# Hybrid RG-LRU / neighbourhood-attention / MoE step: the first expert's down weights are loaded later in the sync engine's queue

## The chip, the cores and the metric

One core of one Trainium2 chip. The metric is the device time of one execution of the whole program, in microseconds (us); the median of several runs is given. The engines are TensorE (PE in the profile, PEld for its weight loads), VectorE (DVE), ScalarE (ACT), GpSimd (POOL) and SyncE (SP), which here only issues DMAs.

## The reference

One layer for 128 context tokens and 512 latent tokens with D_MODEL = 1024, all in float32. The part that matters here is the end, a mixture of 16 experts of which every token uses two:

```python
scores = jax.nn.sigmoid((t @ w_router).astype(jnp.float32))
...
_, idx = lax.top_k(masked, TOP_K)
...
for e in range(N_EXPERTS):
    a = jax.nn.silu(t @ w_exp_gate[e]) * (t @ w_exp_up[e])
    y = y + combine[:, e:e + 1] * (a @ w_exp_down[e])
```

Ahead of it stand adaLN modulation, one input projection, the RG-LRU branch, the attention branch and the merge with its output projection; behind it a gated residual and a final RMSNorm. Gate and up weights of an expert are 1024 x 512, down weights 512 x 1024, so each of the three is 2 MB in float32.

## The kernel before

The program has one stream of instructions for each engine, written out by hand, and semaphores between them. An engine runs its own stream in order, so an instruction that waits holds all that stand behind it.

**Precision.** Every matmul operand is split in two parts: ScalarE makes the high part (a copy to the fp32r type), VectorE or GpSimd the low part (the difference), and TensorE sums three products, high x high, low x high and high x low.

**The expert stage.** The 640 tokens are sorted by expert. A slot tile is 128 rows for one expert. Routing (VectorE, after the output projection) gives each token its slots, and a list idxI of the token in each slot. The normed rows hrow (5 tiles of 128 x 1024) are made by TensorE transposes and ScalarE, get their shift on VectorE (line 1780), and are written by SyncE to h_rows in DRAM (line 543). GpSimd then waits for idxI (idx_ok) and for all five stores (hrow_out) and issues an indirect DMA for each slot tile, which gathers 128 rows of h_rows into one of two buffers hS (line 634 for the first two tiles, line 629 for all later ones). Meanwhile TensorE turns x1 into rows too (line 906), which ScalarE evicts to x1t (line 1257).

**One slot tile on TensorE.** Eight transposes turn hS into columns (line 935), ScalarE takes the high part hSH (line 1268), VectorE the low part hSL (line 1889). Then come the gate product, the up product and, one tile behind, the transposes of the activation (line 956) and the down product; all products are on line 943. For the first tile the gate product is cut in two halves, with the transposes of the second tile's hS between them.

**Expert weights.** Wg, Wu and Wd are one raw buffer each; `load(x, t, ex)` on SyncE waits until VectorE has made the low part of the tile before (W_lo_ok[x] >= t) and then issues one 2 MB DMA; x is 0 for gate, 1 for up, 2 for down. Expert 0's gate weights are loaded earlier, by `first_gate`, in two halves. ScalarE makes the high parts in two pieces of 4 k-tiles each (line 1241), VectorE the low parts in two pieces (line 1883).

**Who reads expert 0's down weights.** On ScalarE the order is: the high part of tile 0's rows, a wait for the row stores, the down weights, then expert 0:

```python
h_high(0, 0)
act.wait_ge(hrow_out, 16 * TT)
weights_high(2, 0)
expert(0, 0, 0)
```

On VectorE it is the low part of the up weights, that of the rows, that of the down weights, then expert 0. The down product of expert 0 itself is taken by TensorE after the up product of expert 1.

Of the kernel before, what the change touches and what calls it, by code (L numbers as in the profile page):

```python
# [106 lines left out]
def build(nc, xT, cT, w_ada, w_ada_late, b_ada, norm_g, final_g, wtiles, par_in, pack, biasd, w_router, r_bias,  # L107
# [235 lines left out]
    def wait(eng, s, v):  # L343

        if not (isinstance(v, int) and v <= 0):
            eng.wait_ge(s, v)
# [72 lines left out]
    def _(sp):  # L419
# [109 lines left out]
        def load(x, t, ex):  # L529

            wait(sp, W_lo_ok[x], t)
            sp.sem_inc(ticks, 1)
            sp.dma_start(Wraw[x][:], experts[bass.ds(ex, 1), x].rearrange("o p (k f) -> (o p) k f", k=KT)) \
                .then_inc(W_in[x], 16)

        sp.wait_ge(half_mm, 2 * (N1 + N2 + N3))
        load(1, 0, 0)
        load(2, 0, 0)
        sp.wait_ge(g2T_ok, 1)
        sp.dma_start(g2d, g2T[0:2 * KT, :]).then_inc(g2_out, 16)  # L540
        for t in range(TT):
            sp.wait_ge(slot_ok, t + 1)
            sp.dma_start(h2d[t * P:(t + 1) * P, :], hrow[:, t, :]).then_inc(hrow_out, 16)
        load(0, 1, 1)
        for x in (1, 2):
            load(x, 1, 1)
        def rows_out(t, b):
# [1504 lines left out]
```

## Time and profile before

| | us |
|---|---|
| median of 3 runs | 1198.25 (1197.57 to 1202.51) |
| time of the profiled execution | 1198.25 |
| its span, first to last instruction | 1196.3 |
| TensorE busy | 1107.3 |
| VectorE busy | 909.7 |
| ScalarE busy | 678.9 |

The profile is of one execution. Times within it are counted from the start of its span; the 1.95 us between time and span lie around the instructions. A busy engine is one that has an instruction in it, and TensorE's busy time includes matmuls that wait in its pipeline. A DMA is seen as its issue on an engine's queue (SPq, POOLq), as its packets, and as its landing, when its semaphore is raised. Queue q1 carries the DMAs that SyncE issues, q0 those that GpSimd issues. The granted clock (PEclk) is a share of 2.4 GHz: 1.00 is that level and 0.50 is 1.2 GHz.

### The profile page before, as it was taken

Reading aid. Unit: us, or ns where it says so; the run is one execution under the profiler, and the core shown is the slowest. Engines: PE = TensorE matmul, PEld = TensorE weight load, DVE = VectorE, ACT = ScalarE, POOL = GpSimd, SP = SyncE. Lnnn points to the kernel's source line nnn. Section 1 sums busy time; section 2 is a strip of 40 time slices with the busy share of each in tenths; the row PEclk is TensorE's granted clock in tenths of the full one; section 3 lists DMA queues with packets and bytes.
Section 4 is the critical chain, followed back from the end, with each engine's and each line's share of the span. In section 5 each row is a group of like instructions: output and inputs, shape, how many; then the busy total and the mean of one; then the engine's idle time right before and its main releaser. Section 6 shows DMA issues by size and latency. Waiting matters only on the chain.

```text
span 1196.3 us, 19808 instructions
## 1 busy us (share of the span) xinstructions
PE 1107.3 (93%) x7082; PEld 1014.9 (85%) x7082; DVE 909.7 (76%) x1255; ACT 678.9 (57%) x1041; POOL 256.1 (21%) x139
## 2 busy tenths in 40 slices
PE   5999999999999999999999999995999999999950
PEld 1599999999999998899999999995788888888840
DVE  6748797978879796866556637558799998999928
ACT  3646757666666756642222212455688877877824
POOL 0132222122222122233333323201110110110011
PEclk9899999999999999999999999997999999999985
DMA  9235412212111221134444445538799999999945
GB/s 366 98 113 160 148 48 81 72 67 84 56 63 57 79 69 50 41 130 152 140 140 141 140 148 192 173 114 316 291 396 421 424 411 418 405 414 427 366 151 200
DMA packets 54569, 232.17 MB, mean 194 GB/s; under 512 B 5328, under 2 KB 22000, under 8 KB 46064
## 3 DMA queue, kind: packets, MB, share of 16 engines
q1 hardware_dynamic: 50480, 216.79, 48.2%
q0 software_dynamic: 4032, 14.68, 3.2%
q8 instruction: 29, 0.48, 0.2%
q14 instruction: 28, 0.23, 0.1%
HBM read 210.45 MB, written 21.00 MB: 193 GB/s over the span
## 4 chain that ended last, share of the span: by engine, by line
PE 50%; DVE 4%; ACT 1%; issue 1%; DMA 1%; POOL 0%; DVEq 0%; SPq 0%; ACTq 0%; POOLq 0%
PE PS L943 24%; PE PS L710 21%; PE PS L935 1%; PE PS L815 1%; PE PS L956 1%; PE PS L860 1%; DVE xo L1947 1%; DVE xo L1949 1%; DVE hrow L1780 0%; PE PS L906 0%; DMA G<-slot_rows,slotI 0%; DVE yo L1959 0%; DVE WgLo L1883 0%; DVE acc L1604 0%; PE PS L848 0%
## 5 line engine op out<-in xcount | busy, mean ns | idle before, releaser
L604 POOL TENSOR_TENSOR wLo<-wRaw,wHi 128x1024 fp32r<-128x1024 f32 x80 | 202.9, 2537 | 547.3 <-ACT wHi L1020 547.2
L710 PE MATMUL PS<-hHi,wHi 128*128 128x320 f32 x896 | 285.2, 318 | 4.3 <-DVE hLo L1435 1.9
L710 PE MATMUL PS<-hLo,wHi 128*128 128x320 f32 x896 | 277.4, 310 | 0.0
L710 PE MATMUL PS<-hHi,wLo 128*128 128x320 f32 x896 | 277.4, 310 | 0.0
L710 PEld LDWEIGHTS PS<-hHi,wHi 128*128 128x128 f32 x896 | 169.4, 189 | 5.6 <-issue 3.2
L710 PEld LDWEIGHTS PS<-hLo,wHi 128*128 128x128 f32 x896 | 169.1, 189 | 0.0
L710 PEld LDWEIGHTS PS<-hHi,wLo 128*128 128x128 f32 x896 | 168.8, 188 | 0.0
L1604 DVE SCALAR_TENSOR_TENSOR acc<-adaL,csil,acc 128x512 f32<-128x512 f32 x112 | 103.8, 985 | 10.3 <-DMA adaL<-in_w_ada_late 9.9
L1020 ACT ACTIVATE wHi<-wRaw 128x1024 fp32r<-128x1024 f32 x80 | 84.1, 1051 | 44.8 <-PE PS L710 44.7
L1883 DVE TENSOR_TENSOR WgLo<-Wg,WgHi 128x2048 fp32r<-128x2048 f32 x34 | 76.4, 2287 | 13.0 <-ACT WgHi L1241 12.9
L1883 DVE TENSOR_TENSOR WdLo<-Wd,WdHi 128x2048 fp32r<-128x2048 f32 x34 | 76.4, 2288 | 9.5 <-ACT WdHi L1241 9.2
L1883 DVE TENSOR_TENSOR WuLo<-Wu,WuHi 128x2048 fp32r<-128x2048 f32 x36 | 80.8, 2286 | 2.6 <-ACT WuHi L1241 2.5
L1459 DVE TENSOR_TENSOR PtLo<-PS,PtHi 128x384 fp32r<-128x384 f32 (+1 forms) x80 | 39.7, 496 | 52.4 <-ACT PtHi L1056 52.3
L1470 DVE TENSOR_SCALAR Sb<-Sb,prec 128x384 f32<-128x384 f32 (+1 forms) x80 | 70.6, 925 | 1.4
L1120 ACT ACTIVATE Sb<-Sb,nmax 128x384 f32<-128x384 f32 (+1 forms) x80 | 45.0, 564 | 46.6 <-DVE nmax L1482 46.5
L1241 ACT ACTIVATE WgHi<-Wg 128x2048 fp32r<-128x2048 f32 x34 | 63.3, 1911 | 11.9 <-DMA Wg<-in_experts 11.8
L1241 ACT ACTIVATE WuHi<-Wu 128x2048 fp32r<-128x2048 f32 x36 | 66.8, 1908 | 3.3 <-DMA Wu<-in_experts 2.0
L1056 ACT ACTIVATE PtHi<-PS 128x384 fp32r<-128x384 f32 (+1 forms) x80 | 35.6, 444 | 56.7 <-PE PS L790 56.0
L626 POOL COPY idxc<-idxI 128x1 int32 (+1 forms) x16 | 20.3, 1269 | 216.5 <-PE PS L935 216.5
L1241 ACT ACTIVATE WdHi<-Wd 128x2048 fp32r<-128x2048 f32 x34 | 63.0, 1905 | 0.0
L943 PE MATMUL PS<-WgHi,hSH 128*128 128x512 f32 x144 | 56.9, 395 | 4.0 <-DVE hSL L1889 2.4
L943 PE MATMUL PS<-WuHi,hSH 128*128 128x512 f32 x144 | 57.8, 402 | 0.0
(324 smaller groups left out, 2764.9 us busy)
## 6 DMA issues: line engine op xcount, KB each, us to landing
wRaw<-in_wtiles SPq DMA_DIRECT2D x80, 512.0 KB, 3.4
Wu<-in_experts SPq DMA_DIRECT2D x18, 2048.0 KB, 9.4
Wg<-in_experts SPq DMA_DIRECT2D x18, 2048.0 KB, 9.7
Wd<-in_experts SPq DMA_DIRECT2D x17, 2048.0 KB
adaL<-in_w_ada_late SPq DMA_DIRECT2D x32, 512.0 KB, 4.3
slot_rows<-Ys SPq DMA_DIRECT2D x18, 512.0 KB, 10.7
ada<-in_w_ada SPq DMA_DIRECT2D x8, 1024.0 KB, 17.7
slot_rows<-tab SPq DMA_DIRECT2D x10, 512.0 KB, 6.5
```

The source lines that it names most:

```text
L604: nc.gpsimd.tensor_tensor(wLo[b][:], wRaw[b][:], wHi[b][:].bitcast(F32), ALU.subtract).then_inc(w_lo, 1)
L626: seq.step(nc.gpsimd.tensor_copy(idxc[b][:], idxI[:, bass.ds(t, 1)]))
L710: r = mm(PS[:, bank, 0:HALF], w[:, k, :], x[:, k, cols], start=(k == 0 and w is wHi[b] and x is xh), stop=(k == KT - 1 and w is wLo[b]))
L943: x = mm(out, lhs[l][:, k, :], rhs[r](k)[:, cols], start=(k == 0 and l == r), stop=(k == n - 1 and l == 1))
L1020: A(wHi[b][:], wRaw[b][:], ACT.Copy).then_inc(w_hi, 1)
L1056: A(PtHi[:, 0:nt, hh * P:(hh + 1) * P], PS[:, 6, 0:nt * P].rearrange("p (t q) -> p t q", q=P), ACT.Copy).then_inc(pt_hi, 1)
L1120: A(Sb[(blk + b) % 2][hh][:, 0:w], Sb[(blk + b) % 2][hh][:, 0:w], ACT.Exp, scale=-1.0, bias=nmax[hh][:], accum_out=psumr[:, hh:hh + 1]).th ...
L1241: A(W_hi[x][:, k:k + 4], Wraw[x][:, k:k + 4], ACT.Copy).then_inc(W_hi_ok[x], 1)
L1459: v.tensor_tensor(PtLo[:, 0:nt, cols], PS[:, 6, 0:nt * P].rearrange("p (t q) -> p t q", q=P), PtHi[:, 0:nt, cols].bitcast(F32), ALU.subtra ...
L1470: v.tensor_scalar(x, x, prec[:, hh:hh + 1], None, ALU.mult).then_inc(prob_ok, 1)
L1604: y = v.scalar_tensor_tensor(acc[:, g, :], w, c1, acc[:, g, :], ALU.mult, ALU.add)
L1883: y = v.tensor_tensor(W_lo[x][:, k:k + 4], Wraw[x][:, k:k + 4], W_hi[x][:, k:k + 4].bitcast(F32), ALU.subtract)
```

## The change

On SyncE, the load of expert 0's down weights, `load(2, 0, 0)`, is issued after the gate load of expert 1 and so after the store of g2 and the five stores of the rows. It was issued right behind the up load of expert 0. No other instruction is changed.

```diff
         sp.wait_ge(half_mm, 2 * (N1 + N2 + N3))
         load(1, 0, 0)
-        load(2, 0, 0)
         sp.wait_ge(g2T_ok, 1)
         sp.dma_start(g2d, g2T[0:2 * KT, :]).then_inc(g2_out, 16)
         for t in range(TT):
             sp.wait_ge(slot_ok, t + 1)
             sp.dma_start(h2d[t * P:(t + 1) * P, :], hrow[:, t, :]).then_inc(hrow_out, 16)
         load(0, 1, 1)
+        load(2, 0, 0)
         for x in (1, 2):
             load(x, 1, 1)
```

## Rows read from the trace of the kernel before

**Rows 1.** The page: TensorE's busy time, share of the span, instructions.

```profile
PE 1107.3 (93%) x7082; PEld 1014.9 (85%) x7082; DVE 909.7 (76%) x1255; ACT 678.9 (57%) x1041; POOL 256.1 (21%) x139
```

**Rows 2.** Busy by stretch: length, PE, PEld, DVE, ACT, POOL, granted clock, DMA share, GB/s.

```profile
815.00:822.00 7.00, 3.24 (x25) 2.91 (x25) 6.30 (x25) 5.53 (x6) 0.30 (x1) 0.74 0.99 369
822.00:827.00 5.00, 4.39 (x21) 3.99 (x19) 4.96 (x7) 3.56 (x6) 3.48 (x2) 0.54 0.53 146
850.00:1140.00 290.00, 290.00 (x1376) 241.22 (x1376) 263.02 (x163) 229.53 (x164) 34.67 (x28) 1.00 0.98 399
```

**Rows 3.** The chain that ended last, 780 to 880 us: start, length, what.

```profile
821.19 5.22 PE PS L906 x24
826.43 0.61 ACT x1t L1257
...
827.08 1.11 PE PS L935 x8
...
830.55 4.34 PE PS L943 x12
834.90 0.88 PE PS L935 x8
...
839.05 1.92 ACT WgHi L1241
...
845.63 5.71 PE PS L943 x24
```

**Rows 4.** Timeline of the SP queue and of POOL, 797 to 850: start, length, what.

```profile
798.17 0.36 SPq L533 DMA_DIRECT2D Wd<-in_experts  x1
...
808.25 6.64 SPq L543 DMA_DIRECT2D h_rows<-hrow  x5
815.00 0.36 SPq L533 DMA_DIRECT2D Wg<-in_experts  x1
827.27 0.33 SPq L533 DMA_DIRECT2D Wu<-in_experts  x1
...
821.70 1.11 POOL L634 DMA_INDIRECT hS<-h_rows,idxI  x1 [36.16 <-DVE idxI L1863]
```

**Rows 5.** Gathers' issue to landing: first; first two; 829.22; 836.81; 14 later.

```profile
DMA to landing us min/median/max: 5.1/5.1/5.1
...
DMA to landing us min/median/max: 5.1/5.6/6.0
...
DMA to landing us min/median/max: 8.2/8.2/8.2
...
DMA to landing us min/median/max: 8.7/8.7/8.7
...
DMA to landing us min/median/max: 9.0/10.9/12.3
```

**Rows 6.** Queues (packets, MB, share): 797:809.3, 815:822.5, 822.5:826, 829:833, 884:888.

```profile
q1 hardware_dynamic: 292, 4.11, 86.2%
...
q1 hardware_dynamic: 302, 2.68, 95.7%
...
q0 software_dynamic: 141, 0.52, 46.7%
...
q1 hardware_dynamic: 87, 1.43, 92.4%
...
q0 software_dynamic: 95, 0.38, 23.1%
```

**Rows 7.** Busy by stretch, columns as in rows 2.

```profile
827.00:830.00 3.00, 1.10 (x8) 0.86 (x8) 0.90 (x2) 1.81 (x3) 0.96 (x2) 1.00 0.74 251
830.00:833.00 3.00, 2.45 (x6) 1.97 (x7) 2.43 (x2) 2.84 (x2) 0.17 (x1) 0.50 1.01 404
```

**Rows 8.** Timeline of ScalarE, 820 to 848; idle before and what ended it.

```profile
829.14 3.70 ACT L1241 ACTIVATE WdHi<-Wd 128x2048 fp32r<-128x2048 f32 x2
835.81 1.03 ACT L1268 ACTIVATE hSH<-PS 128x1024 fp32r<-128x1024 f32 x1 [2.97 <-PE PS L935]
```

## The prediction

> **What bounds the kernel now.** I read first the page's line of TensorE [rows 1]: it is busy for 93% of the span, so what is to be found is where it isn't. The busy times by stretch say where. From 850 to 1140 us, which is nearly the whole expert loop, TensorE is busy 290.0 of 290.0 us and the DMA engines move 399 GB/s; between 815 and 827 us TensorE is far from full and its clock is down [rows 2]. So the loop runs at TensorE's own pace and nothing before it is made up in it: a shift of the first expert by x us is a shift of the end by x us. The question is what the change does to the start of the loop.
>
> The chain of work that ended last shows what sets that start [rows 3]. Routing ends on VectorE and in a few small matmuls; then TensorE transposes x1 (24 in 5.22 us, to 826.41) and ScalarE evicts the last of them until 827.04. Then come the eight transposes of the first tile of gathered rows at 827.08, their high and low parts on ScalarE and VectorE, and the first gate product of expert 0 at 830.55. The gate is done in two halves, with the second gather's transposes between them at 834.90; when it has ended, ScalarE splits the next gate weights from 839.05, VectorE takes their low part, and expert 1 begins at 845.63. Every piece after 827 hangs on the one before it, without a transfer among them.
>
> Beside this chain stands the first gather (hS buffer 0). GpSimd issues it at 821.70 [rows 4] and it takes 5.1 us to land [rows 5], which is 826.8. TensorE takes it up at 827.08, right behind the eviction that ended at 827.04. So gather and eviction end together: the gather has 0.3 us of slack and no more. That is the wait which decides this case.
>
> **The change part by part.** *Taken from 798.17.* The load of expert 0's down weights (2 MB) leaves the first burst. Before, it was issued 0.44 us after the up weights, and h_rows follow from 808.25 [rows 4]. An emptier queue can only make those row stores land sooner. The last is issued at 808.25 + 6.64 - 0.32 = 814.57, and the gather is issued at 821.70, when the token list (idxI) is there; the stores had 7 us. I cost this gain at 0. Even a gather that landed at once would gain only 827.08 - 827.04 = 0.04 us, as the eviction is there.
>
> *Added behind the next gate load.* SP issues the gate load of expert 1 at 815.00; the moved load now follows at about 815.4, with no semaphore to wait for. The next instruction on SP waits for the low part of the up weights and goes out at 827.27 [rows 4] as before, so SP's own queue loses nothing.
>
> *What the transfer does there.* From 815 to 822.5 us queue q1 moved 2.68 MB, which is the last row store and the gate tile, with the engines' share at 95.7% [rows 6]. That is 0.36 MB/us; in a stretch of weights alone (829 to 833) it is 1.43 MB in 4 us, the same. From 797 to 809.3 the up load and the moved one made 4.11 MB [rows 6], over the 10.3 us after the first data (1.3 us behind the issue of 797.7, an estimate) 0.40. The moved 2.10 MB (2048 KB) thus take 2.10/0.40 = 5.2 us behind the gate tile's end at about 822.4, and q1 is full until 827.6. The gather of 821.70 was the one transfer of before that met a queue about to run dry. Now it meets five more microseconds of work.
>
> *The price of that for the gather.* Three kinds of rows bound it. The one before took 5.1 us, which is the lower end (no loss). The second and third gathers after it, issued at 829.22 and 836.81 with one weight tile in flight each, took 8.2 and 8.7 us; the 14 of the loop, where stores of Ys and more than one tile are in flight, took 9.0 to 12.3, median 10.9 [rows 5]. I take the middle of the first two, 8.5, as their load is the nearest: a gather issued some 2 to 6 us ahead of the tile's end. It lands at 821.70 + 8.5 = 830.2 and TensorE's transposes begin there instead of 827.08: +3.1 us. Where these us go is seen from 829 to 833: only q1 moved, 1.43 MB, and not one packet of the gather issued at 829.22 [rows 6], which so stood still for 3.8 of its 8.2 us. Ends for the forecast: a landing at 829.8 (+2.7, the 8.2 rounded down), and 831.4 (+4.3): no packet before q1 runs dry at 827.6, and then the 3.8 us that the first gather took from 823.0, with q1 empty, to its landing at 826.8.
>
> *The clock.* TensorE's granted clock was 1.00 from 827 to 830, where it did 1.10 us of work, and 0.50 from 830 to 833 [rows 7]: the first matmuls of the gate ran at the level of 1.2 GHz. With the gather late TensorE idles 3 us more ahead of the eight transposes. At the low level 24 transposes took 5.22 us [rows 3], so eight take 1.74 against 1.11: +0.6. The gate's first half took 4.34 us for 12 matmuls [rows 3]. In the loop 1376 of them and of the transposes take 290 us [rows 2], 0.21 us each, so 12 take 2.5 at full clock and 5.1 at half: here some 8 were slow. If the fall comes sooner, so may the rise, and two fewer are slow (-0.4); or all 12 are and a few of the second half (+1.0). I take +0.9 for transposes and gate together, with ends of -0.4 and +1.6.
>
> *What stays hidden.* The down weights are first read by ScalarE at 829.14, right behind hSH [rows 8]. They land at about 827.6 plus what the gathers take from them, some 829 to 830, while ScalarE, with the gather late, comes to them at 829.14 + 3.1 = 832.2 or after. Were the gather not late they would cost up to 1 us there, but ScalarE then idled 2.97 us before the next hSH [rows 8]: cost 0. With that cover gone it would be the lateness less 2.97. The second gather took 6.0 us [rows 5] and went out within 2 us of the first, so it landed before 830; it is needed at 834.90 [rows 3], and that moment moves with the first. Four us later is still in time. The up weights of expert 1, issued 827.27, are first read after the gate weights' split, past 843. The copy of g2 is read at the very end.
>
> *Sum.* 3.1 (gather) + 0.9 (clock) - 0 (row stores) = +4.0 us, made against the profiled execution's 1198.25 us (span 1196.3), which is also the median of the three runs: 1202.25, say 1202.2. The forecast's own range is +2.3 (2.7 - 0.4) to +5.9 (4.3 + 1.6), 1200.5 to 1204.2.
>
> The Trainium skill, "DMA: Bandwidth & Descriptors", section "Queues, rings and completion order", says that each DMA engine takes turns between the rows of queues it has work for, a packet at a time. By that rule alone the gather would begin to move at once, between the packets of q1, and not stand still; the third rival gives what this would make. The trace agrees for a gather that has begun (from 884 to 888, 95 packets of q0 passed beside q1's [rows 6]) and not for its first 4 us.
>
> **The rivals.**
> (1) *The gather fares as in the loop.* It would land 10.7 to 12.3 us after its issue, at 832.4 to 834.0: +5.3 to +6.9, with the clock's 0.9 +6.2 to +7.8, that is 1204.5 to 1206. For it: at 821.7 two tiles are queued, not one, the second gather follows in 1.4 us, and the up load of 827.27 begins as the first gather should be catching up. Against: no store of Ys is in flight, and q1 has a gap after 827.6. It decides from 10.5 us between issue and landing. This is the rival of the other side, slower than the measurement's bound.
> (2) *No cost.* The gather's packets go ahead of the moved tile, or that tile's engines are free early; it lands by 827.1: 1198.3. For it: the first gather took 5.1 us though the gate tile was in flight for its first 0.7. Against: all 16 gathers after the first two took 8.2 or more [rows 5], and each had a tile in flight.
> (3) *Turns from the start.* The gather never stands still but shares. From 822.5 to 826 q0 moved 141 packets [rows 6], 40 a us, so the 128 rows of the first gather took 3.2 of its 5.1 us. At the 24 a us of 884 to 888 they take 5.3: 5.1 + 2.1 = 7.2 us, landed at 828.9, +1.8, and with 0.3 for the clock +2.1: 1200.4. For it: the first gather had queue 1's last 0.7 us beside it and lost little. Against: the 4 us without one packet. It decides if packets of q0 are seen before 825.
>
> **How the numbers follow.** About 0.5% (6 us) is what a measurement of this kernel can tell from no change. Forecast 0.56 (of it 0.04 past +6 us); rival 1 0.18 (0.17 past); rival 2 0.12; rival 3 0.10; and 0.04 for what none of them names, of which 0.03 I give to a gain, for which the eviction at 827.04 leaves no room that I can find. With 0.01 of rival 2 this makes faster 0.04, same 0.74, slower 0.22. The predicted time is the forecast's, 1202.2. The range takes in rival 2 below and the greater part of rival 1 above: 1198.0 to 1205.5.
>
> **What would show it.** In the changed kernel's profile: the moved load at about 815.4 on SP; q1 busy until 827 or 828; the first gather with about 8.5 us to landing in place of 5.1, and TensorE's first eight transposes of hS waiting for a DMA, not for ScalarE; the first gate product at about 834 to 835 in place of 830.55; expert 1 at 849 to 850 in place of 845.63; ScalarE not waiting for the down weights; and TensorE full from there. The prediction is wrong if the gather still lands by 827.1, if expert 1's start moves by another amount than the gather, or if the loop makes up the shift.

## The result, and the profile after

The changed kernel takes 1206.29 us (median of 13 runs) against 1199.91 of the kernel before (13 runs): a ratio of 1.0065 with a 95% interval of 1.0048 to 1.0082, so +5.8 to +9.8 us. The two medians are 6.4 us apart, a ratio of 1.0053; the ratio takes in more runs, 39 of the changed kernel with a median of 1207.37. Two further measurements of the same pair gave 1.0063 (1.0037 to 1.0090) and 1.0051 (1.0026 to 1.0076); the kernel before against itself gave 1.0018 (0.9995 to 1.0041) and 1.0011 (0.9984 to 1.0037). Over the three measurements the loss is 6.1 to 7.8 us. Forecast were +4.0 us and 1202.2, with a range up to 1205.5, and slower by over 0.5% had a chance of 0.22.

First the queues' timeline of the changed kernel. All times of this profile stand 3.7 us later than those of before already at the up load (801.47 for 797.73), which is taken up below; so times are read from the first gather's issue.

```profile
811.99 6.64 SPq L542 DMA_DIRECT2D h_rows<-hrow  x5
818.76 0.35 SPq L533 DMA_DIRECT2D Wg<-in_experts  x1
819.22 0.72 SPq L533 DMA_DIRECT2D Wd<-in_experts  x1
830.99 0.33 SPq L533 DMA_DIRECT2D Wu<-in_experts  x1
...
825.42 1.11 POOL L634 DMA_INDIRECT hS<-h_rows,idxI  x1 [36.13 <-DVE idxI L1863]
```

The moved load is where it was looked for, 0.46 us behind the gate load, and 6.2 us ahead of the gather. The next view is the landing of that gather, with the packets of the queues from 825 to 829 (two lines) and from 829 to 833 (two lines).

```profile
DMA to landing us min/median/max: 8.4/8.4/8.4
...
q1 hardware_dynamic: 118, 1.67, 97.6%
q14 instruction: 1, 0.01, 0.5%
...
q1 hardware_dynamic: 66, 0.82, 48.8%
q0 software_dynamic: 197, 0.75, 47.2%
```

The gather was issued at 825.42, and up to 829 there is not one packet of q0: q1 fills the engines to 97.6% with the moved weights. Then q0 passes. It lands after 8.4 us, where it took 5.1 before [rows 5]. The Trainium skill, "DMA: Bandwidth & Descriptors", section "Queues, rings and completion order", has each engine take turns between queues by packets. The trace agrees from 829 on, and not for the 3.6 us before; by turns from the start the forecast had 7.2 us. Not all of the 3.6 us is the moved load's: in the kernel before, where q1 ran dry, the first packet of q0 is seen between 823.2 and 823.7 too, 1.5 to 2 us after the issue.

The chain that ended last now runs through the gather, which was not in it before [rows 3]:

```profile
825.42 8.45 DMA hS<-h_rows,idxI
...
834.01 1.96 PE PS L935 x8
...
838.32 5.40 PE PS L943 x12
843.72 0.87 PE PS L935 x8
...
847.87 1.92 ACT WgHi L1241
...
854.45 5.73 PE PS L943 x24
```

Counted from the gather's issue (821.70 before), TensorE's transposes begin at 8.59 us for 5.38 (+3.21); they take 1.96 for 1.11 (+0.85); the gate's first half takes 5.40 for 4.34 (+1.06); the pieces between are equal to 0.02. Expert 1 begins at 29.03 for 23.93: +5.10. The busy times by stretch, with the columns of [rows 2], show what the second and third terms are:

```profile
834.00:836.00 2.00, 1.94 (x8) 1.55 (x8) 0.00 (x0) 0.02 (x1) 0.00 (x0) 0.50 0.98 414
836.00:838.00 2.00, 0.00 (x0) 0.00 (x0) 0.96 (x1) 2.00 (x2) 1.14 (x2) 0.50 0.96 410
838.00:842.00 4.00, 3.68 (x9) 2.91 (x10) 3.43 (x3) 2.60 (x2) 0.00 (x0) 0.50 0.58 213
842.00:844.00 2.00, 2.00 (x10) 1.56 (x9) 1.33 (x1) 0.00 (x0) 0.00 (x0) 0.63 0.00 0
```

The clock is at 0.50, the level of 1.2 GHz, through both the transposes and nearly all of the gate's first half. Ahead of them TensorE had waited for the gather, with 0.04 us of work from 830 to 834. Before, the clock was 1.00 at the transposes, 0.50 from 830 to 833 [rows 7], 0.80 from 833 to 834 and 1.00 after. ScalarE's timeline answers to [rows 8]:

```profile
836.90 3.70 ACT L1241 ACTIVATE WdHi<-Wd 128x2048 fp32r<-128x2048 f32 x2
844.63 1.03 ACT L1268 ACTIVATE hSH<-PS 128x1024 fp32r<-128x1024 f32 x1 [4.03 <-PE PS L935]
```

It comes to the down weights right behind hSH and waits for nothing; they had landed 13.7 us after their issue, at 832.9. Behind expert 1's start the two profiles run alike: 351.05 us to the end for 350.67. The moved weights are thus not late themselves; they make the gather late.

How much slack the gather had before is less fixed than the 0.3 us of the prediction. In the third of six profiles of the kernel before, issued at the same 821.70, it landed after:

```profile
DMA to landing us min/median/max: 4.4/4.4/4.4
```

The six landings are 4.4, 4.4, 4.5, 4.6, 5.1 and 5.1 us, while TensorE began on it 5.38 or 5.39 us after the issue in five of them: there the eviction of x1 set the start, and the slack was 0.3 to 1.0 us.

### The profile page after: what moved, and what is told of

Its sections match the earlier page's. It is cut to its first block, busy times and chain, and to the rows that moved or that the text cites. A ratio compares the mean times of both kernels' runs of the same rounds, so it can differ in the third digit from the quotient of the medians.

```text
span 1205.5 us, 19808 instructions
## 1 busy us (share of the span) xinstructions
PE 1111.0 (92%) x7082; PEld 1018.0 (84%) x7082; DVE 911.6 (76%) x1255; ACT 679.6 (56%) x1041; POOL 257.6 (21%) x139
## 4 chain that ended last, share of the span: by engine, by line
PE 50%; DVE 4%; DMA 1%; issue 1%; ACT 1%; POOL 0%; DVEq 0%; SPq 0%; ACTq 0%; POOLq 0%
PE PS L943 24%; PE PS L710 21%; PE PS L935 1%; PE PS L815 1%; DMA hS<-h_rows,idxI 1%; PE PS L860 1%; PE PS L956 1%; DVE xo L1947 1%; DVE xo L1949 1%; DVE hrow L1780 0%; DVE yo L1959 0%; DMA G<-slot_rows,slotI 0%; PE PS L848 0%; DVE WgLo L1883 0%; DMA slot_rows<-Ys 0%
```

## The experiments

**The same load one place ahead.** If the down weights' own lateness cost, loading them ahead of the gate weights would help; if the bytes in the queue cost, it would not.

```diff
-        load(0, 1, 1)
         load(2, 0, 0)
+        load(0, 1, 1)
```

> The moved load stands one place ahead: behind the row stores, but before the gate load of expert 1. Queue theory: the same bytes are queued when the gather is issued, so the gather takes 8.0 to 9.0 us and expert 1 begins about 29 us after the gather's issue; ratio 1.004 to 1.008, the same as the changed kernel. Rival (the down weights come too late for ScalarE, which holds the next high parts): they land 5 us earlier here, so the loss should go, ratio 0.998 to 1.002.

Ratio 1.0056 (1.0029 to 1.0082). In the chain:

```profile
822.45 8.21 DMA hS<-h_rows,idxI
...
830.80 1.96 PE PS L935 x8
...
851.57 3.00 PE PS L943 x12
```

The gather takes 8.2 us and expert 1 begins 29.12 us after its issue. The order of the two loads makes no difference in these profiles; that both are in the queue when the gather comes is common to them.

**The same load behind the gather's landing.**

```diff
         load(0, 1, 1)
+        sp.wait_ge(hs_in[0], 16)
         load(2, 0, 0)
```

> As the changed kernel, but SyncE waits for the landing of the first gather before it issues the load of the down weights (and with it the up load of expert 1). The down weights land later still, at about 833 us on the clock of the kernel before. Queue theory: the gather meets only the gate tile and takes 5 us, TensorE's transposes begin 5.4 us after its issue, and ScalarE's wait for the down weights, some 4 us, is covered by the 4.7 us that it idles before the tanh of the gate: expert 1 begins 23.9 to 24.5 us after the gather's issue, ratio 0.999 to 1.002. Rival (late down weights cost): the loss is as large as in the changed kernel or larger, ratio 1.004 or above, with ScalarE waiting for Wd and the first gate product on time.

Ratio 1.0037 (1.0013 to 1.0061). The chain, and below it ScalarE's timeline:

```profile
824.82 4.31 DMA hS<-h_rows,idxI
...
829.21 8.29 DMA Wd<-in_experts
...
850.30 6.58 PE PS L944 x21
...
837.59 3.73 ACT L1242 ACTIVATE WdHi<-Wd 128x2048 fp32r<-128x2048 f32 x2 [5.23 <-DMA Wd<-in_experts]
```

The queue's part came out: without the moved tile the gather takes 4.3 us, and TensorE's transposes begin 5.38 us after its issue, to the hundredth as before. The rest of my expectation was wrong by a piece. The down weights took 8.3 us to land, not the 5.2 of their bytes, ScalarE waited 5.23 us for them, and expert 1 began at 25.48 for 23.93 us, 1.55 late. ScalarE's idle time of 4.7 us is not a full cover: VectorE's low part of the down weights (4.49 us) then stands in front of its work for the next rows and gate weights, and holds the chain. So down weights that keep ScalarE waiting for 5.23 us cost 1.55 us. The changed kernel does not reach it. The ratio, +1.6 to +7.3 us, is above the 0.999 to 1.002 expected, and it can't tell the two theories apart: its profile had 352.7 us from expert 1 to the end and the stall that is taken up below. What speaks for the queue is the stage.

**Half of it.** K-tiles 0 to 3 of the down weights in the old place, 4 to 7 in the new. ScalarE's waits are set to match (not shown).

```diff
         load(1, 0, 0)
-        load(2, 0, 0)
+        sp.dma_start(Wraw[2][:, 0:4], experts[0, 2].rearrange("p (k f) -> p k f", k=KT)[:, 0:4]) \
+            .then_inc(Wl_in, 16)
...
         load(0, 1, 1)
+        sp.dma_start(Wraw[2][:, 4:8], experts[0, 2].rearrange("p (k f) -> p k f", k=KT)[:, 4:8]) \
+            .then_inc(W_in[2], 16)
```

> Half of the down weights (k-tiles 0 to 3, 1 MB) is loaded in the old place, half in the new. Queue theory: q1 runs dry 2.6 us after the gate tile's end and not 5.2; the gather stands still until its packets' turn and takes 6.5 to 8 us; expert 1 begins 26 to 27.5 us after the gather's issue; ratio 1.002 to 1.005. If a gather always stands still for its 4 us whenever any tile is queued behind the running one, it takes 8 us as with the whole tile, and the ratio is that of the changed kernel. Rival (late down weights): the second half still lands before ScalarE comes to it, ratio 1.000.

Ratio 1.0038 (1.0014 to 1.0062).

```profile
822.65 5.79 DMA hS<-h_rows,idxI
...
828.57 1.08 PE PS L938 x8
...
832.01 5.49 PE PS L946 x12
...
848.41 5.72 PE PS L946 x24
```

The gather takes 5.8 us, less than the 6.5 to 8 expected, and TensorE begins on it 0.54 us later than before. Half of the bytes cost a sixth of the delay (0.54 for 3.21), so the gather does not wait in proportion to the bytes. The time at which q1 runs dry fits better. After the gather's issue q1 still moved 0.25 MB in the kernel before, until some 1.5 us after it, 1.2 MB here, until about 4, and 2.2 MB in the changed kernel, until about 7. The last two gathers land 1.5 to 2 us after that. The half load's q1 is dry before even a gather with nothing beside it has landed (4.4 us, in a run below), so its bytes cost little. This is read from three profiles, and no run tests it. Of the loss of 1.83 us at expert 1, 1.15 are the gate's first half, 5.49 us for 4.34: the slow clock once more. But the kernel before has 5.49 in one of its six profiles too, so this part can't be put down to the half load.

**Keeping TensorE busy.** Transposes of the identity are added where TensorE waits, into PSUM columns that nobody reads. The third of the four places, ahead of the first gather's transposes, is used in the changed kernel only.

```diff
+        def warm(n, bank):
+            for _ in range(n):
+                nc.tensor.transpose(PS[:, bank, 0:P], C("ident"), C("ident"))
...
         to_rows(0, xa, range(2 * TT))
+        warm(36, 0)
...
         to_rows(1, x1, range(4))
+        warm(14, 0)
...
         pe.wait_ge(tr_ev, 4 * TT)
+        warm(36, 4)
...
         h_cols(0, 0, 16)
+        warm(14, 4)
         expert(0, 0, 16)
```

> The changed kernel, with transposes of the identity added on TensorE where it waits: 36 behind the first transposes to rows, 14 ahead of the inverse list, 36 before the first gather's transposes, 14 between these and the first gate product; they write PSUM columns that nobody reads. Clock theory: of the changed kernel's loss 0.9 us in the eight transposes and 1.1 in the gate's first half come from the low clock at the restart; here the granted clock stays 1.00, the eight transposes take 1.1 us, the first 12 gate matmuls under 3.2, and expert 1 begins 25 to 26.5 us after the gather's issue instead of 27.3 to 29.1; ratio to the kernel before 1.001 to 1.004. Rival (the whole loss is the gather's landing, the clock's share is noise): expert 1 at 28 to 29, ratio 1.006. The gather itself must stay at 8 to 9 us by both.

Ratio 1.0026 (1.0003 to 1.0049).

```profile
823.24 8.84 DMA hS<-h_rows,idxI
...
832.12 1.11 PE PS L943 x8
...
835.59 3.02 PE PS L951 x12
...
849.34 5.73 PE PS L951 x24
```

The gather is as late as ever (8.8 us), but the transposes take 1.11 us and the 12 matmuls 3.02. Expert 1 begins 26.10 us after the gather's issue where the changed kernel has 27.30 to 29.44. Against a kernel before that has no such transposes, what is left is 2.2 us: the gather's +3.5 less the 1.3 that the gate gains.

> The kernel before with the same transposes of the identity, save the 36 that stand before the first gather's transposes. Clock theory: the first 12 gate matmuls take under 3.2 us instead of 4.3 and the transposes of x1 run at full clock, so that the gather alone ends the wait: expert 1 begins 22 to 23 us after the gather's issue, 1 to 2 us sooner, ratio 0.998 to 1.000. Rival: no gain, 23.9 us as before, as the added transposes hold TensorE up when the rows come.

Ratio 0.9995 (0.9975 to 1.0014), which is no difference that can be told.

```profile
827.40 1.11 PE PS L942 x8
...
830.87 3.06 PE PS L950 x12
...
844.65 5.69 PE PS L950 x24
```

Expert 1 begins 22.64 us after the gather's issue for 23.93, so 1.3 us are gained in the stage, as expected of the gate (3.06 for 4.34). The transposes of x1 did not get faster, against the expectation: 24 in 5.22 us as before. The gain is below what the ratio can show.

Set side by side, these two kernels give the price of the moved load with the low clock out of both: expert 1 at 26.10 for 22.64 us, +3.46, and TensorE's start on the gather at 8.88 for 5.39, +3.49. So the gather is all that is left of the loss, and what the changed kernel lost beyond it was the clock.

> As before_warm, and SyncE issues expert 1's gate load only when the first gather has landed, so that the gather meets no weight tile at all. Queue theory: the gather takes 4.0 to 4.5 us instead of 5.1, and expert 1 begins another 0.5 to 0.8 us sooner if the gate weights, which then land some 8 to 9 us after their issue at about 826, are there when ScalarE comes to them 17 us after the gather's issue. Ratio 0.997 to 1.000. Rival: they are late for ScalarE, and expert 1 begins at 24 us or later.

Ratio 1.0003 (0.9984 to 1.0021). SyncE waits here for the first gather before it loads expert 1's gate weights.

```profile
820.42 4.36 DMA hS<-h_rows,idxI
...
842.61 11.67 DMA Wg<-in_experts
...
862.72 7.34 PE PS L951 x24
```

The gather takes 4.4 us, which is no gain: it took 4.5 in the run above. Expert 1 begins at 22.2 us, 0.4 sooner still, and that comes from elsewhere. TensorE begins on the gather 4.50 us after its issue for 5.39, as the granted clock was 1.00 from 820 to 824.9 and the transposes of x1 ended sooner; then the 14 added transposes held the gate up by 0.8 us. Later the gate weights of expert 2 take 11.7 us to land, and the chain goes through that DMA: from expert 1's start to the end it is 356.9 us for 350.7. This is one profile, and the ratio shows neither gain nor loss. Why that load took 11.7 us stays open.

**Is the stage's loss the whole loss?** The stage lost 5.1 us in the profile, and the ratio stands for 5.8 to 9.8. The changed kernel's profile had come to the stage 3.7 us late. Followed back by the times of SyncE's loads, 3.2 of these were lost between 326 and 379 us, in the attention loop, which the change does not touch. The waits of the stretch from 300 to 400 us, and the instruction queue's packets over the whole span:

```profile
PE PS L710 <- issue: 2.7, 1, 2.7
...
ACT PtHi L1056 <- issue: 2.8, 1, 2.8
...
q8 instruction: 38, 0.62, 0.2%
```

TensorE and ScalarE stand still for 2.7 and 2.8 us and wait for nothing that the profile shows, and 38 instruction packets were moved where the kernel before had this:

```profile
q8 instruction: 29, 0.48, 0.2%
```

That looks like a wait for instructions, which no run here shows beyond these packets. To see whether it goes with the change, both kernels were run again, unaltered.

> The changed kernel once more, unaltered, for a second profile. Queue theory (the first gather stands behind the moved 2 MB, and TensorE's clock is low when it restarts): gather 8.0 to 9.0 us from issue to landing, TensorE's first transposes of hS 8.2 to 9.2 us after the gather's issue (5.4 in the kernel before), the 12 matmuls of the gate's first half 5 us or more, expert 1 begins about 29 us after the gather's issue (23.9 before); ratio 1.004 to 1.008. Rival (chance: the 3.7 us that the first profile of the changed kernel had lost before the change's place, in a stall of TensorE and ScalarE near 357 us, belong to the change too): the stall is there again at the same place and of the same length. If it is chance it is absent or elsewhere.

> The kernel before, unaltered, against itself, for a second profile of it and for what the ratio does between equal kernels. Ratio 0.9975 to 1.0025. If the stall of 3 us near 357 us, with nine more instruction packets on q8 (38 for 29), is chance and not the change's, it is to be seen in some executions of this kernel too. The stage of the change as in the first profile: gather 4.8 to 5.5 us, expert 1 begins 23.5 to 25.5 us after the gather's issue.

> The changed kernel a third time. So far its stage lost 5.1 and 3.4 us against the kernel before, and the ratio says 7.8 and 7.5. Open is whether the rest is chance from before the stage (stalls ahead of 797 us). If the change costs what the stage shows: expert 1 begins 27.3 to 29.2 us after the gather's issue, gather 8.0 to 8.9 us; ratio 1.003 to 1.008. If the stall of 3 us in the stretch 300 to 400 belongs to the changed kernel it is there a third time.

> The kernel before a third time, against itself: expert 1 begins 23.9 to 24.0 us after the gather's issue, ratio 0.998 to 1.002. If the stall of 3 us in the stretch 300 to 400 is chance it may be seen here; if it belongs to the changed kernel it is not.

> The changed kernel a fourth time, one profile: expert 1 begins 27.3 to 29.2 us after the gather's issue; with the stall in 300 to 400 or without it, as after_third.

> The kernel before a fourth time, one profile: expert 1 begins 23.9 to 24.0 us after the gather's issue; without the stall if it belongs to the changed kernel.

> A further profile of the changed kernel. Chance theory: the stall of 3 us near 357 us, with 38 instruction packets on q8, comes and goes in both kernels. Theory that it goes with the change: it is here (3 of 4 profiles so far), not in the kernel before (0 of 4). The change's own stage by both: expert 1 begins 27.3 to 29.5 us after the gather's issue.

> A further profile of the kernel before. Chance theory: the stall near 357 us is seen here sooner or later. Theory that it goes with the change: it is not here. The stage by both: expert 1 begins 23.9 to 24.1 us after the gather's issue.

> The changed kernel once more, with the same two theories of the stall near 357 us as for after_fifth: by chance it is here or not, by the other theory it is here. Expert 1 begins 27.3 to 29.5 us after the gather's issue.

> The kernel before once more, with the same two theories of the stall as for before_fifth: by chance it is here or not, by the other theory it is not. Expert 1 begins 23.9 to 24.1 us after the gather's issue.

Six profiles of each kernel, the first ones with them, in us:

| | gather's issue | TensorE begins on it, from its issue | expert 1, from the issue | expert 1 to the end | span | stall near 357 |
|---|---|---|---|---|---|---|
| before | 821.70 | 5.38 | 23.93 | 350.67 | 1196.3 | no |
| before_again | 823.76 | 5.38 | 23.97 | 351.27 | 1199.0 | no |
| before_third | 821.70 | 5.38 | 23.98 | 351.02 | 1196.7 | no |
| before_fourth | 819.68 | 5.39 | 24.06 | 350.56 | 1194.3 | no |
| before_fifth | 824.16 | 5.38 | 24.04 | 350.60 | 1198.8 | no |
| before_sixth | 826.87 | 5.24 | 25.15 | 352.28 | 1204.3 | yes |
| changed | 825.42 | 8.59 | 29.03 | 351.05 | 1205.5 | yes |
| after_again | 826.82 | 8.10 | 27.30 | 350.88 | 1205.0 | yes |
| after_third | 826.44 | 8.75 | 29.44 | 352.32 | 1208.2 | yes |
| after_fourth | 822.20 | 8.83 | 29.38 | 351.12 | 1202.7 | no |
| after_fifth | 825.90 | 8.15 | 27.36 | 350.84 | 1204.1 | yes |
| after_sixth | 825.90 | 8.66 | 29.37 | 352.33 | 1207.6 | yes |

The means of the spans are 1198.2 and 1205.5, which are 7.3 us apart, as the ratios say. Of these, 4.5 are the stage (28.65 for 24.19 from the issue to expert 1), 2.5 are the time before the gather's issue (825.45 for 822.98) and 0.4 the time after expert 1 has begun. Of the stage's 4.5, 3.15 are the gather (8.51 for 5.36) and 1.3 the clock. The 2.5 go with the stall: without it the gather's issue is at 822.20 in the changed kernel's one profile and 822.20 in the mean of the other's five; with it at 825.42 to 826.82 in the changed kernel and 826.87 in the other.

The stall is in the kernel before too, in its sixth profile:

```profile
PE PS L710 <- issue: 2.5, 1, 2.5
...
q8 instruction: 38, 0.62, 0.2%
```

So it is not made by the change alone. It was in 5 of 6 profiles of the changed kernel and 1 of 6 of the other. Of the other experiments' profiles only the one with the load behind the gather had it; those with the load ahead of the gate load, with half a load and the three with added transposes did not. Whether the change makes it more frequent stays open. In profiles without it the spans are 1202.7 (one) and 1197.0 (mean of five), +5.7.

The stage varies as well, mostly by the clock. Two changed profiles have 27.3, and one of them shows this:

```profile
826.82 7.96 DMA hS<-h_rows,idxI
...
834.92 1.76 PE PS L935 x8
...
839.04 4.36 PE PS L943 x12
```

The gate's first half took 4.36 us here and 5.40 in the first profile, and in the kernel before's sixth it took 5.49 (25.15 us to expert 1), for 4.34 in the first.

## Why the prediction was wrong, point by point

- **What bounds the kernel: right.** The gather and the eviction of x1 stood side by side, and no part of the shift was made up in the loop. The slack of 0.3 us was that of one profile; in the others it was up to 1.0 us, and the eviction was what TensorE waited for.
- **The gain from the row stores, 0: right.** They landed sooner and nothing moved.
- **The gather, +3.1: right.** 8.5 us to landing were taken from the gathers beside one tile; it was 8.0 to 8.7 in six profiles, and TensorE began on it 3.15 us later on average. The first rival's 10.7 us or more was seen in none, and the third rival's 7.2 us neither. The second rival, no cost, is out. The reason given for the price is weaker than the price: 8.5 was the middle of two other gathers' times, and the landing is not in proportion to the bytes, as the half load showed. Of the 3.8 us of standing still, 1.5 to 2 are there with q1 all but empty.
- **What stays hidden: right here.** ScalarE never waited for the down weights. Further out my reckoning of the cover is off: with ScalarE at them 5.33 us late the rule of the prediction, lateness less 2.97, gives 2.4, the 4.7 of the expectation 0.6, and 1.55 were lost.
- **The clock, +0.9 with ends of -0.4 and +1.6: too small for the first profile, right in kind.** It was +1.9 there (0.85 in the transposes, 1.06 in the gate), +1.3 on average. I took a middle between a clock that rises sooner and one that stays low through both; in four of six profiles, those with 29.0 us or more to expert 1, it stayed low. With TensorE kept busy the 1.9 us went away. The 2.5 us reckoned for the 12 matmuls at full clock were too low, as 0.21 us each is a mean that takes in the shorter transposes: they took 3.02 and 3.06. By its own sign of being wrong, expert 1's start moving by another amount than the gather, the prediction fails too (4.5 us for 3.15), though its sum had the clock beside the gather.
- **The sum, +4.0 on 1198.25 us, is where it failed: what lies outside the stage was put at nothing.** The stage lost 4.5 us on average, within the forecast's own range of +2.3 to +5.9; the half microsecond above the sum is the clock. The sum took the profiled execution for all executions, in two ways. It let its 1198.25 us stand for the kernel before, whose 13 runs have a median of 1199.91: that is 1.7 us of the 4.1 by which the time was missed. And it assumed that nothing ahead of the stage differs, where the changed kernel came to the gather 2.5 us later on average. That difference is the stall near 357 us, which was in five of six profiles for one of six; why it comes, and whether the change brings it more often, stays open. (The parts are means of six profiles, whose spans are 7.3 us apart, and the medians are 6.4 apart, so they add up to somewhat more than 4.1.) The range ended at 1205.5 because only the first rival's landing reached past it, and spread between executions had no part in it, though the three runs shown were up to 5 us apart.

## What to carry to other kernels

A load that is moved "to where there is room" must be judged by what is issued while its bytes are on their way: here one gather with 0.3 to 1.0 us of slack met 2 MB, and what went beyond the slack was passed on in full. Price such a transfer by rows of the same transfer issued beside as much traffic, and add the clock for every wait of TensorE that grows. And where a run-to-run spread of several us is seen in three runs, put it in the range: a stage known to half a microsecond says little of a median.

## What the runs showed of the hardware

- A gather issued on q0 behind two loads of q1 moved no packet for 3.6 us, and then ran beside q1. It landed in 8.0 to 8.8 us with 2.2 MB of q1 still to move (the changed kernel), in 5.8 with 1.2 MB (the half load), in 4.3 to 5.1 with some 0.25 MB, and in 4.4 with none.
- Two DMAs of 2 MB, issued 0.46 us apart, landed after 8.4 and 13.7 us in the changed kernel. One issued with q1 empty and the second gather still on its way took 8.3, though its bytes alone need 5.2 at the prediction's 0.40 MB a us.
- The same twelve matmuls took 4.34 to 5.49 us in six profiles of one and the same program, and 3.02 and 3.06 with TensorE kept busy ahead of them. A stall of TensorE of 2.5 to 3.3 us with nine more instruction packets came in 6 of 12 executions of the two kernels. The spans of the kernel before were from 1194.3 to 1204.3 in six profiles.
